# Three gate units and the output product of the second layer as high and low parts, in a two-block transformer kernel on one core

## The reference

```python
h = _rmsnorm(x, norm_g[1])
proj = h @ o_w_in                       # q_c, k and v of three branches, gates, z_c, q_d, k_d, v_d, z_d
o_c = _nsa_attention(qc, ...)           # compressed, selected and window branches, gated
y_c = _merge_heads(o_c) * silu(z_c)
o_d = _banded_attention(qd, kd, vd, ..., sinks)
y_d = _merge_heads(o_d) * silu(z_d)
x = x + concat([y_c, y_d]) @ w_out[1]   # 1024x1024: "wo1"
```

## Time and profile before

| | |
|---|---|
| median of three runs | 909.28 us |
| profiled execution | 910.96 us, span 909.2 us, mean granted clock 0.994 |
| TensorE busy | 882.9 us, 97% |
| GpSimd busy | 609.0 us, 67% |
| ScalarE, VectorE busy | 446.7 us, 428.8 us |
| attention steps of layer 2 | 213.9 to 293.4 us |
| rest of wo1 | 293.4 to 314.0 us |
| norm with ak2_0, ak2_1 | 314.0 to 326.7 us |

### The profile page before, as it was taken

How to read it: one execution, slowest core, us unless ns; L and a number is a source line. 1 busy time by engine, 2 the same in 40 slices (tenths; PEclk the granted TensorE clock), 3 DMA queues, 4 the chain that set the end, 5 groups by cost and what they waited for, 6 DMA issues and landing times.

```text
span 909.2 us, 16515 instructions
## 1 busy us (share of the span) xinstructions
PE 882.9 (97%) x6792; PEld 826.0 (91%) x6792; DVE 428.8 (47%) x952; ACT 446.7 (49%) x665; POOL 609.0 (67%) x485
## 2 busy tenths in 40 slices
PE   6999999899999999999999999999999999999997
PEld 5898889897777999888988799999999999999996
DVE  3998665743875466882445232331124562211001
ACT  3434667344555453354444547586334775533330
POOL 0766468740000669989777777768889999997880
PEclk9999999999999999999999999999999999999999
DMA  9844577783210279597666444444536655545421
GB/s 347 344 146 158 214 243 266 252 307 131 100 48 1 93 275 391 219 376 261 226 213 232 149 176 145 154 167 156 216 139 232 231 185 187 185 141 186 185 94 47
DMA packets 27907, 177.61 MB, mean 195 GB/s; under 512 B 3080, under 2 KB 5780, under 8 KB 7480
## 3 DMA queue, kind: packets, MB, share of 16 engines
q1 hardware_dynamic: 26248, 174.35, 53.1%
q10 hardware_dynamic: 1584, 2.20, 0.7%
HBM read 174.95 MB, written 3.43 MB: 196 GB/s over the span
## 4 chain that ended last, share of the span: by engine, by line
PE 90%; DVE 4%; ACT 2%; issue 1%; DMA 1%; POOL 1%; ACTq 0%; DVEq 0%; SPq 0%
PE proj L742 18%; PE proj L744 18%; PE proj L745 18%; PE proj L717 5%; PE proj L822 3%; PE proj L819 3%; PE proj L821 3%; PE proj L1016 3%; PE proj L778 2%; PE mixed L968 1%; PE proj L1089 1%; PE transposed L937 1%; PE scores L923 1%; PE mixed L951 1%; PE sums L876 1%
## 5 line engine op out<-in xcount | busy, mean ns | idle before, releaser
L656 POOL TENSOR_TENSOR w_lo<-raw,w_hi 128x512 fp32r<-128x512 f32 x328 | 418.9, 1313 | 208.2 <-ACT w_hi L1374 208.1
L744 PE MATMUL proj<-parts,w_lo 128*128 128x256 f32 x952 | 266.4, 280 | 0.6 <-POOL w_lo L656 0.6
L742 PE MATMUL proj<-parts,w_hi 128*128 128x256 f32 x904 | 257.3, 285 | 0.5 <-POOL w_lo L656 0.3
L745 PE MATMUL proj<-parts,w_hi 128*128 128x256 f32 x904 | 252.6, 279 | 0.0
L1374 ACT ACTIVATE w_hi<-raw 128x2048 fp32r<-128x2048 f32 x82 | 156.8, 1914 | 112.4 <-DMA raw<-in_weights 61.0
L744 PEld LDWEIGHTS proj<-parts,w_lo 128*128 128x128 f32 x952 | 179.1, 188 | 1.7 <-POOL w_lo L656 0.8
L742 PEld LDWEIGHTS proj<-parts,w_hi 128*128 128x128 f32 x904 | 169.9, 188 | 2.8 <-issue 2.1
L745 PEld LDWEIGHTS proj<-parts,w_hi 128*128 128x128 f32 x904 | 170.4, 188 | 0.0
L656 POOL TENSOR_TENSOR w_lo<-arena,w_hi 128x512 fp32r<-128x512 f32 (+2 forms) x44 | 56.2, 1317 | 56.5 <-ACT w_hi L1374 56.5
L742 PE MATMUL proj<-hid_hi,w_hi 128*128 128x256 f32 x160 | 45.3, 283 | 0.0
L819 PE MATMUL proj<-w_hi,parts 128*128 128x512 f32 x112 | 45.0, 402 | 0.0
(11 more groups left out here) (402 smaller groups left out, 2111.7 us busy)
## 6 DMA issues: line engine op xcount, KB each, us to landing
raw<-in_weights SPq DMA_DIRECT2D x105, 1024.0 KB, 5.0
arena<-in_weights SPq DMA_DIRECT2D x32, 1024.0 KB, 7.2
wide<-in_weights SPq DMA_DIRECT2D x9, 1024.0 KB, 7.0
probT<-in_weights SPq DMA_DIRECT2D x8, 1024.0 KB, 5.6
dil_lines<-dil_line SPq DMA_DIRECT2D x1, 2304.0 KB, 12.9
prob<-in_weights SPq DMA_DIRECT2D x2, 1024.0 KB, 4.9
dil_bias<-dil_lines SPq DMA_DIRECT2D x1, 1536.0 KB, 9.4
xT<-in_x SPq DMA_DIRECT2D x2, 512.0 KB, 5.8
```

Source lines behind the costliest of these rows:

```text
L656: nc.gpsimd.tensor_tensor(lo_slots[RAW_AT[n]][:, at], raw_slots[RAW_AT[n]][:, at], hi_slots[HI_AT[m]][:, at].bitcast(F32), ALU.subtract).t ...
L742: nc.tensor.matmul(dst, whi, h, start=first, stop=False)
L744: nc.tensor.matmul(dst, wlo, h, start=False, stop=False)
L745: last = nc.tensor.matmul(dst, whi, lo[:, k, :], start=False, stop=stop)
```

## The change

zc1, zd0, zd1 and wo1_0 to wo1_3 join `SPLIT` and are multiplied as parts. Their high copies stand at given places on ScalarE ("L:hi_..." in steps 0, 2, 3, 5, 8 and 12; zc1's is made by `passing` ahead of the steps), and `passing` stops at a unit with a given place. The wo1 units and ak2_0, ak2_1 may take a fourth high place, in `dil_bias`, which the plain zc0 reads until it is done. The raw units wo1_0 and later may use all seven places, and ak2_0, ak2_1 and rq0 are no longer loaded ahead of wo1_2 and wo1_3. y is split as well: pieces 0 and 1 (y_c) by "L:y0" and "L:y1" in steps 12 and 13, pieces 2 and 3 (y_d) at the end. In steps 13 and 14 TensorE multiplies y's piece 0, then 1, by the rows of wo1_0 and wo1_1 that meet them ("H:0", "H:1"), and behind the steps pieces 2 and 3, then wo1_2 and wo1_3 whole. A memset on GpSimd moves from ahead of ak2_0 to ahead of zc1.

```diff
--- before.py
+++ after.py
@@ -61,8 +61,9 @@
 FILL_CD = [x.split() for x in (
-    "N:kd E:zc0", "zc1.0 E:kd", "zc1.1", "E:zc1", "modA zd0.0.0", "zd0.0.1 E:modA", "", "zd0.1", "zd1.0 E:zd0", "", "zd1.1.0",
-    "zd1.1.1", "", "H:wo1_0 E:zd1", "H:wo1_1", "")]
+    "N:kd E:zc0 L:hi_zd0", "zc1.0 E:kd", "zc1.1 L:hi_zd1", "E:zc1 L:hi_wo1_0", "modA zd0.0.0", "zd0.0.1 E:modA L:hi_wo1_1", "",
+    "zd0.1", "zd1.0 E:zd0 L:hi_wo1_2", "", "zd1.1.0", "zd1.1.1", "L:y0 L:hi_wo1_3", "H:0 E:zd1 L:y1", "H:1", "")]
+PLACED = ("zd0", "zd1", *(f"wo1_{i}" for i in range(4)))
 HEAD_B, HEAD_CD = ["bv1", "sp_bk1", "zb0"], ["vc2", "zc0", "sp_kd"]
@@ -156,7 +157,7 @@
 
-SPLIT_SOON = ["bq1", "bk0", "bk1", "bv0", "bv1", "zb0", "zb1", "za0", "za1"] + [f"wo0_{i}" for i in range(4)] + ["kcvc", "kskw", "vsvw", "qc0", "qc1", "vdgt", "qd0", "qd1", "kd"]
+SPLIT_SOON = ["bq1", "bk0", "bk1", "bv0", "bv1", "zb0", "zb1", "za0", "za1"] + [f"wo0_{i}" for i in range(4)] + ["kcvc", "kskw", "vsvw", "qc0", "qc1", "vdgt", "qd0", "qd1", "kd", "zc1", *PLACED]
 SPLIT = [u for u in WEIGHTS if u in SPLIT_SOON or WEIGHT_AT[u] >= WEIGHT_AT["ak2_0"] and u[:2] != "ad"]
@@ -194,18 +195,19 @@
         return range(NRAW + sum(n >= WEIGHT_AT[start] for start in RAW_MORE))
-    return EARLY if n >= WEIGHT_AT["wo1_0"] else [*range(NRAW), *EARLY]
+    return [*range(NRAW), *EARLY]
 
 
 RAW_AT, RAW_BEFORE = take_slots(WEIGHTS, raw_slots_of)
-HI_AT, HI_BEFORE = take_slots(SPLIT, lambda n, u: range(NHI + sum(n >= SPLIT_AT[start] for start in HI_MORE)))
+SHARED_HI = SPLIT[SPLIT_AT["wo1_0"]:SPLIT_AT["ak2_1"] + 1]
+HI_AT, HI_BEFORE = take_slots(SPLIT, lambda n, u: [*range(NHI), NHI + 1] if u in SHARED_HI else range(NHI + sum(n >= SPLIT_AT[start] for start in HI_MORE)))
 
 LATE_BEFORE = ("rv3b", "ak0_1", "aq1_1", "ak1_1", "aq2_0", "av0b", "av1a", "av1b")
 LATE_AFTER = ("rk3", "rv3:1", "aq0_0", "ak0_0", "aq1_0", "ak1_0", "ak1_1", "aq2_0")
 FIRST_BEFORE = ("ck0", "qd0", "cv1", "qd1")
 FIRST_AFTER = ("wo0_3", "kskw", "qc0", "qc1")
 LOADS = [u for u in WEIGHTS if u not in ADA_FIRST + ADA_VECTOR + ADA_LATE]
-for _us, _before in ((BEFORE_NORM["x2"], "wo1_2"), (("rq0",), "wo1_3"), *(((u,), before) for u, before in zip(ADA_FIRST, FIRST_BEFORE)), *(((u,), before) for u, before in zip(ADA_LATE, LATE_BEFORE)),
+for _us, _before in (*(((u,), before) for u, before in zip(ADA_FIRST, FIRST_BEFORE)), *(((u,), before) for u, before in zip(ADA_LATE, LATE_BEFORE)),
                      *(((u,), before) for u, before in zip(ADA_VECTOR, ("rk0", "rk1", "rk2", "rk3", "rv0a", "rv2a", "rv2b", "rv3a")))):
@@ -662,7 +664,7 @@
                             .then_inc(sem("h0_low"), 1)
-                if u == "ak2_0":
+                if u == "zc1":
                     pool.wait_ge(proj_ready, GROUP_AT["hidv"] + 1)
@@ -988,7 +990,8 @@
                 elif name[:2] == "H:":
-                    output_half(name[2:], 0, yT1, y_of)
+                    n = int(name[2:])
+                    state["pair"] = two_units(("wo1_0", "wo1_1"), gathered(n, n + 1), state["pair"] if n else None, done=False)
                 elif name == "L:mean":
@@ -1000,9 +1003,9 @@
 
-            def output_half(name, half, y, piece):
-
-                plain(name, y, piece, range(KD // 2 * half, KD // 2 * (half + 1)), fresh=half == 0, done=half == 1)
+            def gathered(lo, hi):
+
+                return [((2 * n, 2 * n + 1), every, lambda k, n=n: pe.wait_ge(y_ready, 4 + n + 1)) for n in range(lo, hi)]
 
@@ -1170,7 +1173,6 @@
 
-            y_of = lambda k: pe.wait_ge(po_free, STEPS_TO["b"] + 2 * (k // 2) + 2) if k % 2 == 0 else None
             def convolved_product(i):
@@ -1251,10 +1253,10 @@
 
-                if i < 2:
-                    output_half(f"wo1_{i}", 1, yT1, y_of)
-                else:
-                    plain(f"wo1_{i}", yT1)
+                if i == 0:
+                    two_units(("wo1_0", "wo1_1"), gathered(2, 4), state["pair"])
+                elif i > 1:
+                    project(f"wo1_{i}")
 
@@ -1324,14 +1326,14 @@
                 if name[1] == "r":
-                    wait = (lambda k: pe.wait_ge(y_ready, 4 + k // 2 + 1)) if i == 0 else None
+                    wait = (lambda k: pe.wait_ge(y_ready, 8 + k // 2 + 1)) if i == 0 else None
                     features(name, None, yret_lo, [[(f"{name}{x}", 0, 0)] for x in "ab"], wait)
                 else:
                     pe.wait_ge(po_free, STEPS_TO["a"])
                     features(name, att_hi, att_lo, [[(f"wa{i // 2}", 256 * (i % 2) + P * j, 0)] for j in range(2)])
             def merged_product(i):
                 if i == 0:
-                    ready = lambda k: pe.wait_ge(y_ready, 12 + k // 2 + 1)
+                    ready = lambda k: pe.wait_ge(y_ready, 16 + k // 2 + 1)
                     two_units(("wo2_0", "wo2_1"), [(range(6), every, ready), (range(6, KD), every, ready)])
@@ -1355,25 +1357,29 @@
 
-            def passing(name, most=len(SPLIT)):
-
-                while state["hi"] < min(len(SPLIT), most):
+            def passing(name, placed=None):
+
+                while state["hi"] < len(SPLIT):
                     m = state["hi"]
                     v = SPLIT[m]
                     n = WEIGHT_AT[v]
-                    old = GROUP_AT["wr0"] - 1 if v in HI_MORE else -1 if HI_BEFORE[m] is None else LAST_READ[SPLIT[HI_BEFORE[m]]]
+                    if v in PLACED and v != placed:
+                        break
+                    old = GROUP_AT["wr0"] - 1 if v in HI_MORE else GROUP_AT["zc0"] if v == SHARED_HI[0] else -1 if HI_BEFORE[m] is None else LAST_READ[SPLIT[HI_BEFORE[m]]]
                     loaded = LOADED_AFTER[v] + (v != "kskw") if v in SPLIT_SOON else max(LOADED_AFTER[v], GROUP_AT["wo1_0"] - 1)
-                    if max(old, loaded) >= GROUP_AT[name]:
+                    if placed is None and max(old, loaded) >= GROUP_AT[name]:
                         break
                     kt, w = unit_shape(v)
-                    if HI_BEFORE[m] is not None:
-                        act.wait_ge(proj_ready, LAST_READ[SPLIT[HI_BEFORE[m]]] + 1)
-                    elif v in HI_MORE:
+                    if v in HI_MORE:
                         act.wait_ge(po_free, STEPS_TO["a"])
+                    elif old >= 0:
+                        act.wait_ge(proj_ready, old + 1)
                     act.wait_ge(raw_in[RAW_AT[n]], raw_target(n))
                     nc.scalar.activation(hi_slots[HI_AT[m]][:, 0:kt * w], raw_slots[RAW_AT[n]][:, 0:kt * w], ACT.Copy) \
                         .then_inc(hi_ready, 1)
                     state["hi"] += 1
+                    if placed is not None:
+                        break
 
@@ -1472,7 +1478,11 @@
                         fl((yT0 if name[1] == "b" else yT1)[:, (0 if name[1] == "c" else 4) + 2 * i:][:, 0:2])
-                    nc.scalar.activation(dst, ready(name)[:], ACT.Tanh, scale=0.5).then_inc(sem("z_tanh"), 1)
+                    nc.scalar.activation(dst, ready(name, name not in PLACED)[:], ACT.Tanh, scale=0.5).then_inc(sem("z_tanh"), 1)
+                elif name[:5] == "L:hi_":
+                    passing(name[5:], name[5:])
+                elif name[:3] == "L:y":
+                    gathered_high(int(name[3:]))
                 elif name == "L:centre":
@@ -1496,6 +1506,10 @@
                     copy_out(name, fl((gaT if name[1] == "a" else gbT)[:, 2 * i:2 * i + 2]), fn=ACT.Sigmoid)
+
+            def gathered_high(n):
+
+                operand_high([(hi_of(n), two(yT1, n), [(proj_ready, GROUP_AT["zd1"] + 1), (po_free, STEPS_TO["b"] + 2 * n + 2)])])
 
@@ -1670,6 +1684,8 @@
             narrow_attention(PART["c"] + PART["d"], FILL_CD)
+            for n in (2, 3):
+                gathered_high(n)
             table(ACT.Sqrt)
@@ -1971,6 +1987,8 @@
                     keys_out("sp_kd", "kd", kdT, "d_knorm_g")
+                elif name[:3] == "L:y":
+                    parts_low(yT1, [int(name[3:])])
                 elif name == "L:centre":
@@ -2272,7 +2290,8 @@
             normalise(PART["c"][0])
-            narrow_attention(PART["c"] + PART["d"], FILL_CD, 1)
+            narrow_attention(PART["c"] + PART["d"], FILL_CD, 1, lambda: parts_low(yT1, [2]))
+            parts_low(yT1, [3])
 
```

## The result

The changed kernel took 917.07 us (median of five runs, 916.62 to 917.29), the kernel before beside it 909.67 (907.03 to 910.65): ratio 1.0088, 95% interval 1.0071 to 1.0105. It is slower by 0.9%. The forecast was 910.5 us and "no change"; the time lies at the upper edge of the range, just outside it (904 to 917). The two profiled executions took 917.07 and 910.96 us, so between the profiles there are 6.1 us to explain.

A forecast was written before the change was run, and what follows sets the result against it. TensorE, 97% busy, was taken to bound most of the kernel, but to wait on the VectorE and ScalarE chain in the attention steps. +1.0 + 2.3 + 1.7 - 3.8 = +1.2 gave 912.2 profiled, 910.5 us as median; range 904 to 917.

The forecast's parts named there:

- steps 0 to 11 without contention: Attention steps 0 to 11: shorter gate products end step 12's mixing 1.4 us earlier, 2.4 of 3.8 us lost to waits.
- contention there: Steps 0 to 11: three normalisings slowed by GpSimd's low parts, up to 3 us; end of step 12's mixing taken as +1.0.
- steps 12 to 15, clock apart: Last attention steps: y's low parts and wo1_3's copy delay normalising and mixing, +2.3 us, at most +2.9.
- clock: Attention steps: longer TensorE idle stretches drop the granted clock once more, +1.7 us, bounds -1.7 to +5.1.
- wo1's rest: Output product behind the attention steps: 48 shorter products, -3.8 us, y2's and y3's parts adding no wait.
- the 0.73 us row: A 128x512 normalising beside GpSimd's low parts that took 0.73 us, almost unchanged; cited for no contention.
- rival C: Every idle stretch of some 1.6 us drops the clock, with full contention: +5.8 us, 915.1 us; chance 0.20.
- M: End of the mixing in step 12; step 13's transposes were forecast at M+3.4, the last mixing's end at M+16.95.
- Products: Seven units, 112 products as parts: 0.079 us less each, 8.8 us less TensorE work.
- rival D: Behind wo1, late weights (ak2_0, ak2_1 or rq0) keep TensorE waiting, price 2 to 4 us, 914 us; chance 0.04.
- rival A: Whole kernel: TensorE's work alone counts, -8.8 us, 900.5 us; chance 0.06.
- Rival B: Same waits, without contention or further clock falls: 904.4 to 906.1 us; chance 0.24.

The follow-up runs named there:

- memset_prompt: Changed kernel with zeros for six units' low parts, y0 and y1 low parts behind the normalisings and wo1_3's high copy in step 14: 906.9 us, ratio 0.9975.
- fillers: Changed kernel with four extra float32 matmuls into an unused bank ahead of TensorE's wait in seven steps: 915.99 us, ratio 1.0100.
- y_prompt: Changed kernel with y0 and y1 low parts made behind the normalisings of steps 13 and 14, wo1_3's high copy in step 14: 915.55 us, ratio 1.0065.
- gates_only: Kernel before with only zc1, zd0 and zd1 multiplied as parts, wo1 plain: 911.95 us, ratio 1.0018.
- quarter_prompt: Changed kernel with six units' low sets in 16 pieces instead of 4, and y_prompt's order: 909.04 us, ratio 0.9996.

## Why the prediction was wrong

Between the profiles, by the prediction's own terms:

| term | predicted | measured |
|---|---|---|
| steps 0 to 11 without contention | -1.4 | -0.4 (memset_prompt against before, step 12) |
| contention there | +2.4 | +7.5 (fillers against memset_prompt, step 12) |
| steps 12 to 15, clock apart | +2.3 | +3.0 (17.80 against 14.76, after against before) |
| clock | +1.7 | -0.4 (+1.3 at 251 to 257, the fall at 274 gone: -1.7) |
| wo1's rest | -3.8 | -3.7 |
| sum | +1.2 | +6.0 (6.1 between the executions) |

**The step that failed is the contention of steps 0 to 11.** The mechanism was named, and its price per instruction, "0 to 1.0 us", held to 0.1 us: the large normalising at 236.49 took 1.1 us more, the gate multiplication at 232.05 0.8. What was wrong is the count. I charged three normalisings, those of steps 3, 9 and 10; four of 512 or 1024 columns were held, of steps 3, 6, 7 and 10. And I left the instructions of 128x4 at nothing. Eight of these and one of 128x60 took 0.88 to 1.27 us each in steps 0 to 11, and they lie in the same chain as the normalising that follows them. Together the thirteen took 12.3 us more than undisturbed, of which 7.5 reached the end of the stretch. The prediction even held the sentence that counts them: the Trainium skill, page "SBUF — State Buffer", section "Who interferes with whom", by which an instruction with two SBUF inputs and a GpSimd one that reads SBUF exclude each other for a whole instruction, gave an estimate of 1 us for each tiny gate multiplication. The rows of this case agree with it for the five that a set overlapped (0.97, 1.10, 0.97, 1.11, 1.09 us, where 0.16 is undisturbed), and I let no term follow from it. I had taken the 0.73 us row of 128x512 for a sign that such instructions are spared; 1.75 and 1.72 us for the same shape in steps 6 and 7 show that they are not. A wait that lasts until a piece ends is sometimes almost nothing, so one fast row bounds nothing. The same page of the Trainium skill says that tensor_scalar can take the shared ports as well, and reductions not. The trace agrees: L1919 went from 159 to 645 ns and the 1.22 us reduction stayed.

**The bound was too low for the same reason.** The upper end of the term was "up to 3 us, end of mixing +1.6"; the measured one is -0.4 + 7.5 = +7.1. TensorE's idle time in the stage shows the same: "some 11 us" was forecast, and 17.6 were measured. So rival C, which has the right sign and the nearest time (915.1), has it in part by the wrong route: "It decides from two further falls on", and two came, but the falls gave nothing on balance. That the time lies only just outside the range is luck of the same kind: the range was wide enough for the falls of C, and contention filled it.

**Steps 0 to 11 without contention: nearly right.** -1.4 was forecast, -0.4 measured. memset_prompt was 0.9 us ahead of the kernel before at the transposes of step 4 and 0.6 behind at those of step 6; in this stretch stands the copy of wo1_1, behind that of wo1_0. That the copies do it is argued, not shown: no run leaves them out alone.

**Steps 12 to 15: right in kind and place.** Predicted: transposes of step 13 at M+3.4. Measured: M = 285.08 (282.68 + 2.40), transposes at 288.63, M+3.55. The last mixing ended at M+18.1 where M+16.95 stood. Of the 3.0 us at most 0.5 is contention: the held 128x4 row at 292.57 and TensorE's wait of 0.52 us behind it. The other 2.5 are the order, where I had 1.95.

**The clock: right in kind, wrong in sum.** More falls were expected, and two came; that one in step 13 "hides under VectorE's wait" held to 0.1 us. What I priced at 1.7 was worth 1.3, and the old fall went away. The length of a wait alone does not decide whether a fall follows: ahead of step 12, 1.58 us in the kernel before and 1.89 in y_prompt had one behind them, 1.90 at the same place in the kernel after and in gates_only had none. Which stretches fall differs from kernel to kernel (see the table), so a single fall is not a property of the change.

**Products, wo1's rest and the later stages: right.** 48 products behind the steps in 16.9 us; 3.7 us less; no weight came late, so rival D did not happen. In the steps the 64 shorter products are there too (TensorE busy 66.1 us in quarter_prompt, where no fall stretches it, against 74.4 before with its falls), but the steps are bound by VectorE's chain and give none of it back. That is why rival A was far off. Rival B's 904.4 to 906.1 is close to what the kernel without low sets and with the better order gives, 906.9.

## What to carry to other kernels

Before moving work to an idle GpSimd, list every VectorE instruction of the kinds that were held here (tensor_tensor with both inputs in SBUF, tensor_scalar) in the stretch beside it, the tiny ones too: each can wait for the GpSimd instruction in progress, so the cost is at most their number times the length of one piece. If the work must stand there, cut it into short pieces (16 in place of 4 took the loss at step 12 from 8.8, 1.3 of it clock, to 1.2 us); better, put it where VectorE's chain doesn't set the end. Where an engine is 97% busy over the whole program but waits in one stage, take the saving only from the stretch that has no gaps: 32 products there were worth more than 112 everywhere.

## What the runs showed that I had not expected

A 128x4 instruction of 0.16 us took 0.88 to 1.27 us beside a low set; the two whose pieces were worked out above ended with the piece. Cutting the set into 16 pieces costs GpSimd 1.7 us per set (6.75 against 5.01) and was worth it against whole pieces. The granted clock stayed at 0.50 for 6.8 us from 250.9 us on, twice as long as the fall at 288.5 (3.4 us), with another wait (1.56 us) inside. And filling TensorE's waits to hold the clock up bought 1.3 us in the steps of the profiled execution, but no gain in time that the runs could tell.
